# A gated delta rule in pairs of heads: the next pair's projection, issued one product at a time in other places of TensorE's order

## The reference

```python
# per head, with chunks of 128 tokens
A = jnp.where(strict, einsum(k_beta, kc) * L, 0.0)
sol = lax.linalg.triangular_solve(eye + A, rhs, lower=True, unit_diagonal=True)
u, w = sol[..., :dv], sol[..., dv:]
attn = jnp.where(causal, einsum(qc, kc) * L, 0.0)
def step(S, inp):
    v_new = u_n - w_n @ S
    o = q_n @ S + a_n @ v_new
    S = S * d_n + k_n.T @ v_new
    return S, o
...
do = do * lax.rsqrt(jnp.mean(do * do, axis=-1) + EPS) * dn_norm_g[l]
do = do.reshape(B, T, DN_V) * jax.nn.silu(dz)
y_dn = do @ w_dn_br[l]
merged = jax.nn.sigmoid(gate_r) * y_ret + jax.nn.sigmoid(gate_d) * y_dn
h = h + merged @ w_o[l]
```

## Time and profile before

| | us |
|---|---|
| median of 3 runs | 2510.35 (2509.15 to 2514.41) |
| profiled execution | 2510.26 |
| its span | 2508.3 |
| TensorE busy | 2352.5 (94%) |
| VectorE, ScalarE, GpSimd busy | 1132.0, 851.0, 871.7 |

### The profile page before, as it was taken

The page is one execution under the profiler, slowest core; times in us unless marked ns, Lnnn a source line. Parts: engine busy times, 40 slices in busy tenths (PEclk is TensorE's granted clock), DMA queues, the critical chain, the costliest instruction groups (busy, mean ns, idle before and its releaser), DMA issues.

```text
span 2508.3 us, 28287 instructions
## 1 busy us (share of the span) xinstructions
PE 2352.5 (94%) x11226; PEld 1908.3 (76%) x11226; DVE 1132.0 (45%) x1490; ACT 851.0 (34%) x844; POOL 871.7 (35%) x382
## 2 busy tenths in 40 slices
PE   7999999989899999999998999999997889999897
PEld 5888787757567788888776778878796867788786
DVE  7322007746644632200725416463737445877502
ACT  4222214357443422221426424141414033333312
POOL 3444343423213344434432434141322123344343
PEclk9999999999999999999999999999999889999998
DMA  4322223322322323222321132121111023222222
GB/s 137 97 88 92 84 92 90 87 56 69 108 73 71 108 86 99 92 76 95 108 78 57 60 101 84 34 72 46 48 54 59 26 98 110 87 92 92 67 92 76
DMA packets 161873, 203.23 MB, mean 81 GB/s; under 512 B 11949, under 2 KB 116728, under 8 KB 161784
## 3 DMA queue, kind: packets, MB, share of 16 engines
q1 hardware_dynamic: 155008, 197.16, 24.8%
q10 hardware_dynamic: 6775, 4.80, 0.6%
HBM read 191.45 MB, written 10.49 MB: 81 GB/s over the span
## 4 chain that ended last, share of the span: by engine, by line
PE 59%; issue 16%; DVE 15%; ACT 5%; POOL 4%; DMA 0%; SPq 0%; POOLq 0%; DVEq 0%; ACTq 0%
PE PS L167 15%; PE PS L168 15%; PE PS L169 15%; POOL wl L158 4%; DVE cv L2045 2%; PE PS L1911 2%; PE PS L1920 1%; DVE h_lo L310 1%; PE PS L1919 1%; PE PS L194 1%; PE PS L195 1%; PE PS L196 1%; PE PS L1007 1%; DVE work L2088 1%; DVE work L2078 1%
## 5 line engine op out<-in xcount | busy, mean ns | idle before, releaser
L158 POOL TENSOR_TENSOR wl<-raw,wh 128x2048 fp32r<-128x2048 f32 (+1 forms) x214 | 805.8, 3766 | 1487.3 <-ACT wh L149 1487.3
L167 PE MATMUL PS<-h_hi,wh 128*128 128x512 f32 x1696 | 680.1, 401 | 23.1 <-DVE h_lo L310 8.7
L169 PE MATMUL PS<-h_hi,wl 128*128 128x512 f32 x1696 | 666.6, 393 | 0.0
L168 PE MATMUL PS<-h_lo,wh 128*128 128x512 f32 x1696 | 666.1, 393 | 0.0
L149 ACT ACTIVATE wh<-raw 128x2048 fp32r<-128x2048 f32 (+1 forms) x214 | 340.0, 1589 | 935.1 <-PE PS L169 874.2
L167 PEld LDWEIGHTS PS<-h_hi,wh 128*128 128x128 f32 x1696 | 322.3, 190 | 104.1 <-issue 9.6
L169 PEld LDWEIGHTS PS<-h_hi,wl 128*128 128x128 f32 x1696 | 321.7, 190 | 69.2
L168 PEld LDWEIGHTS PS<-h_lo,wh 128*128 128x128 f32 x1696 | 322.7, 190 | 63.9 <-issue 0.7
L167 PE MATMUL PS<-act_hi,wh 128*128 (+1 forms) x528 | 210.0, 398 | 7.9 <-POOL wl L158 6.6
L616 DVE SCALAR_TENSOR_TENSOR xT<-PS,xT 128x512 f32<-128x512 f32 x40 | 27.4, 685 | 407.4 <-PE PS L169 407.3
L168 PE MATMUL PS<-act_lo,wh 128*128 (+1 forms) x528 | 209.5, 397 | 0.0
(11 more groups left out here) (439 smaller groups left out, 3114.9 us busy)
## 6 DMA issues: line engine op xcount, KB each, us to landing
raw<-in_w_in_dram SPq DMA_DIRECT2D x104, 512.0 KB, 4.7
raw<-in_w_up_dram SPq DMA_DIRECT2D x88, 512.0 KB, 4.8
raw<-in_w_down_dram SPq DMA_DIRECT2D x132, 256.0 KB, 2.8
raw<-in_w_gate_dram SPq DMA_DIRECT2D x44, 512.0 KB, 3.9
raw<-in_w_out_dram SPq DMA_DIRECT2D x16, 256.0 KB, 2.7
raw<-in_w_ret_br_dram SPq DMA_DIRECT2D x8, 512.0 KB, 4.8
gates<-stage SPq DMA_DIRECT2D x16, 256.0 KB, 5.5
raw<-in_w_dn_br_dram SPq DMA_DIRECT2D x8, 512.0 KB, 4.6
```

The source lines that it names most:

```text
L158: nc.gpsimd.tensor_tensor(wl[:, slot, 0:size], raw[:, slot, 0:size], wh[:, slot, 0:size].bitcast(F32), ALU.subtract).then_inc(w_lo, 1)
L167: nc.tensor.matmul(dst, sh, mh, start=start, stop=False)
L168: nc.tensor.matmul(dst, sh, ml, start=False, stop=False)
L169: return nc.tensor.matmul(dst, sl, mh, start=False, stop=stop)
```

## The change

`next_panel` takes a number of products and keeps its own place in the panel, so a k-step can be split. The 32 products of pairs 0 to 2 are dealt out as 2 in each of the six levels, 2 before `u`, 5 behind it, 1 before each of chunk steps 1 to 3, 7 behind the last chunk step and 3 behind `oT`. The second half of the pair's second panel is split by `panel_b`: 4 products before the wait on `silA`, 12 behind its transposes. In pair 3, 24 products of the branch product are dealt out (before: 16): 6 before the wait on `T0`, 1 in each level, 1 before `u`, 3 behind it, 1 before each of chunk steps 2 and 3, 6 behind the last. The units of `w_dn_br` come in another order (all of banks 0 to 3 first), and `merge2b_pe` has 40 products left: 4 behind `oy`, 36 behind `olo`. ScalarE rounds unit u+8 (in pair 3 ub+2) behind `uev` instead of before `u`, and u+9 behind `ohi` instead of behind `uev`.

```diff
--- before.py
+++ after.py
@@ -1716,17 +1716,30 @@
 
     def merge2b_sp(sp):
         for v in range(4):
-            panel(sp, ub + v, A['w_dn_br_2'][0], 4 * (v // 2), 4, 512 * (v % 2))
+            panel(sp, ub + v, A['w_dn_br_2'][0], 4 * (v % 2), 4, 512 * (v // 2))
             if v == 2:
                 wide_store(sp, WIDE - 1)
 
     def merge2b_pe(pe):
 
         await_point(pe, "dve", 3, "oy")
-        unit_T(pe, ub + 1, (ub + 1) % 2, 4, 0, 4, do_hi, do_lo, True, False)
+        branch_part(pe, ub + 2, 4, 0, 1)
         await_point(pe, "dve", 3, "olo")
-        unit_T(pe, ub + 2, (ub + 2) % 2, 0, 4, 4, do_hi, do_lo, False, True)
-        unit_T(pe, ub + 3, (ub + 3) % 2, 4, 4, 4, do_hi, do_lo, False, True)
+        branch_part(pe, ub + 1, 0, 6, KD)
+        branch_part(pe, ub + 2, 4, 1, 4)
+        branch_part(pe, ub + 3, 4, 4, KD)
+
+    def branch_part(pe, u, bank, k0, k1):
+
+        if k0 % 4 == 0:
+            pe.wait_ge(w_lo, u + 1)
+        for k in range(k0, k1):
+            for m in range(4):
+                c0 = (k % 4) * 512 + m * P
+                ins = mm3(PS[:, bank + m, :], wh[:, u % 2, c0:c0 + P], wl[:, u % 2, c0:c0 + P], do_hi[:, k, :], do_lo[:, k, :],
+                          k == 0, k == KD - 1)
+        if k1 % 4 == 0:
+            ins.then_inc(w_used, 1)
 
     def merge2b_load(act):
 
@@ -1762,7 +1775,7 @@
             dve.tensor_tensor(part, part, sig_r[:, 4 * n:4 * n + 4, :], ALU.mult).then_inc(g_mul, 1)
         for n in range(2):
             dve.wait_ge(g_sig, SIG1 + 3 + n)
-            dve.wait_ge(w_used, ub + 3 + n)
+            dve.wait_ge(w_used, ub + 2 + 2 * n)
             for m in range(4 * n, 4 * n + 4):
                 dve.tensor_tensor(sig_d[:, m, :], sig_d[:, m, :], PS[:, m, :], ALU.mult).then_inc(g_mul, 1)
             for m in range(4 * n, 4 * n + 5):
@@ -1853,12 +1866,13 @@
                 unit_T(pe, u + 1, (u + 1) % 2, 0, 4, 4, h_hi, h_lo, False, True)
                 pe.wait_ge(M1_copied, 2)
             unit_T(pe, u + 2, u % 2, 4, 0, 4, h_hi, h_lo, True, False)
+            panel_b(pe, u + 3, 4, 5)
             await_point(pe, "act", pp, "silA")
             for a in range(4):
                 for c in range(NT):
                     ins = pe.transpose(tile_of(PS, a, c), tile_of(cv, a, c), ident[:, :])
             at_point(ins, "pe")
-            unit_T(pe, u + 3, (u + 1) % 2, 4, 4, 4, h_hi, h_lo, False, True)
+            panel_b(pe, u + 3, 5, KD)
             await_point(pe, "dve", pp, "qn")
             for a, src in ((0, wE), (2, wkd)):
                 for e in range(2):
@@ -1899,9 +1913,11 @@
                 pe.wait_ge(fl_ev, GATES + q - KD + 2)
                 wide_mm(pe, q + 3, 3, 0, KD)
 
-            await_point(pe, "dve", pp, "T0")
             pe.wait_ge(fl_ev, GATES + q - KD + (4 if pp < 3 else 2))
             await_point(pe, "act", pp, "aT")
+            if pp == 3:
+                next_panel(pe, pp, 6)
+            await_point(pe, "dve", pp, "T0")
             for l, b in enumerate(LEVELS):
                 n = 2 * (len(LEVELS) * pp + l)
                 for e in range(2):
@@ -1910,7 +1926,7 @@
                     for c in range(NT):
                         ins = mm(tile_of(PS, 4 + e, c), tile_of(wAT, e, c), tile_of(wT, e, c), start=True, stop=True)
                     ins.then_inc(d_X, 1)
-                next_panel(pe, pp, l)
+                next_panel(pe, pp, 2 if pp < 3 else 1)
                 for e in range(2):
                     pe.wait_ge(d_Xm, n + e + 1)
                     for c in range(NT):
@@ -1920,7 +1936,7 @@
                         ins = mm(PS[:, 6 + e, 256 + lo:256 + hi], tile_of(wX, e, c), halves(tile_of(wU, e, c), b)[1],
                                  start=True, stop=True)
                     ins.then_inc(d_TU, 1)
-            next_panel(pe, pp, 6)
+            next_panel(pe, pp, 2 if pp < 3 else 1)
             pe.wait_ge(d_Um, 2 * len(LEVELS) * (pp + 1))
             pe.wait_ge(d_scaled, 3 * (pp + 1))
             for e in range(2):
@@ -1928,10 +1944,12 @@
                     mm(tile_of(PS, 4 + e, c), tile_of(wU, e, c), tile_of(wvb, e, c), start=True, stop=True)
                     ins = mm(tile_of(PS, 6 + e, c), tile_of(wkb, e, c), tile_of(wU, e, c), start=True, stop=True)
             at_point(ins, "pe")
-            next_panel(pe, pp, 7)
+            next_panel(pe, pp, 5 if pp < 3 else 3)
             await_point(pe, "act", pp, "uev")
             for c in range(NT):
                 if c:
+                    if pp < 3 or c > 1:
+                        next_panel(pe, pp, 1)
                     for e in range(2):
                         pe.wait_ge(d_S, 2 * (3 * pp + c - 1) + e + 1)
                         mm(PS[:, 6 + e, 0:P], tile_of(wAT, e, c), Sst[:, e, :], start=True, stop=True).then_inc(d_wS, 1)
@@ -1943,27 +1961,44 @@
                         mm(PS[:, 6 + e, P:2 * P], tile_of(wkd, e, c), tile_of(wX, e, c), start=True, stop=True).then_inc(d_kv, 1)
                     ins = mm(tile_of(PS, 4 + e, c), tile_of(waT, e, c), tile_of(wX, e, c), start=c == 0, stop=True)
             at_point(ins, "pe")
+            next_panel(pe, pp, 7 if pp < 3 else 6)
             await_point(pe, "dve", pp, "on")
             for e in range(2):
                 for c in range(NT):
                     ins = pe.transpose(tile_of(PS, 6 + e, c), tile_of(wT, e, c), ident[:, :])
             at_point(ins, "pe")
-
-    def next_panel(pe, pp, k):
-
-        if pp == 3 and k >= 4:
-            return
-        u = ud + 6 * pp + 6 + k // 4 if pp < 3 else ub
+            if pp < 3:
+                next_panel(pe, pp, 3)
+
+    def panel_b(pe, u, k0, k1):
+
+        if k0 == 4:
+            pe.wait_ge(w_lo, u + 1)
+        for k in range(k0, k1):
+            for m in range(4):
+                c0 = (k % 4) * 512 + m * P
+                ins = mm3(PS[:, 4 + m, :], wh[:, u % 2, c0:c0 + P], wl[:, u % 2, c0:c0 + P], h_hi[:, k, :], h_lo[:, k, :],
+                          k == 0, k == KD - 1)
+        if k1 == KD:
+            ins.then_inc(w_used, 1)
+
+    panel_at = [0, 0, 0, 0]
+
+    def next_panel(pe, pp, n):
+
         mh, ml = (h_hi, h_lo) if pp < 3 else (do_hi, do_lo)
-        if k % 4 == 0:
-            pe.wait_ge(w_lo, u + 1)
-        if pp == 3 and k % 2 == 0:
-            await_point(pe, "dve", k // 2, "olo")
-        for m in range(4):
+        for _ in range(n):
+            k, m = panel_at[pp] // 4, panel_at[pp] % 4
+            panel_at[pp] += 1
+            u = (ud + 6 * pp + 6 if pp < 3 else ub) + k // 4
+            if m == 0 and k % 4 == 0:
+                pe.wait_ge(w_lo, u + 1)
+            if pp == 3 and m == 0 and k % 2 == 0:
+                await_point(pe, "dve", k // 2, "olo")
             c0 = (k % 4) * 512 + m * P
             ins = mm3(PS[:, m, :], wh[:, u % 2, c0:c0 + P], wl[:, u % 2, c0:c0 + P], mh[:, k, :], ml[:, k, :], k == 0, k == KD - 1)
-        if k % 4 == 3:
-            ins.then_inc(w_used, 1)
+            if m == 3 and k % 4 == 3:
+                ins.then_inc(w_used, 1)
 
     def delta_pool(pool):
         los(pool, ud, 4)
@@ -2016,14 +2051,10 @@
                 wide_out(act, q + 2, 2)
                 wide_out(act, q + 3, 3)
                 rounds(act, u + 7, 1)
-                rounds(act, u + 8, 1)
-            else:
-                rounds(act, ub + 2, 1)
             await_point(act, "pe", pp, "u")
             act.activation(wX, PS[:, 4:6, :], ACT.Copy)
             at_point(act.activation(wAT[:, :, :], PS[:, 6:8, :], ACT.Copy), "act")
-            if pp < 3:
-                rounds(act, u + 9, 1)
+            rounds(act, u + 8 if pp < 3 else ub + 2, 1)
             await_point(act, "pe", pp, "o")
             if pp == 3:
                 merge2b_load(act)
@@ -2032,6 +2063,8 @@
             at_point(act.activation(ssq[:, 0:8], ssq[:, 0:8], ACT.Sqrt), "act")
             await_point(act, "dve", pp, "oy")
             at_point(act.activation(do_hi[:, 2 * pp:2 * pp + 2, :], wU, ACT.Copy), "act")
+            if pp < 3:
+                rounds(act, u + 9, 1)
 
     def conv(dve, pp, lo, hi, src):
```

## The result

| | us |
|---|---|
| before, median of 4 runs | 2510.61 (2509.15 to 2514.41) |
| changed, median of 4 runs | 2479.06 (2478.05 to 2479.84) |
| changed, profiled execution and its span | 2479.08, 2477.2 |

The ratio of the runs is 0.9872, with a 95% interval from 0.9855 to 0.9889: 31.5 us faster. The forecast was 2483 us, 27.7 us faster, with a range from 2474 to 2494.

The account below looks back on a forecast made before the run. TensorE's work plus its idle or half-clock stretches was taken to bound the kernel. Three boundaries 18.6, pair 0 -0.6, pair 3 15.3 and clock -5.6 sum to 27.7 us off 2510.35: 2483 us, range 2474 to 2494.

Parts of the forecast that it names:

- TensorE's stalls are filled by products that cover nothing where they stood: Pairs 0 to 2: products leave the levels and fill waits at the boundary, 6.2 us gained for each of three boundaries.
- From `oT` to `qn` nothing changes: Pair boundaries: VectorE's and ScalarE's steps set `qn`, a fixed 13.65 us behind the `silA` transposes; moving products out gains nothing.
- The split saves at `silA` what it pays at `qn`: The 2.56 us stall goes, idle before `qn` grows from 0.75 to about 3.5 us: zero; pair 0 loses 0.6 us.
- The clock behind the new gap: Behind `qn`: a 3.5 us idle gap, four times, brings half clock, 4 x 1.4 = 5.6 us lost.
- the rival in which the clock holds: Behind `qn`: the clock stays full through the new gaps; 2477 us, chance 0.24.
- GpSimd beside the convolution: nothing: Boundaries: GpSimd's subtraction beside the convolution costs zero, bounded above by 4.5 us per boundary.
- Pair 3: Last pair: 8.2 us gained up to its end, 5.6 from fewer products behind it, 1.45 from half clock; 15.3 us together.
- 2504 us: No-change rival: half clock behind each new gap lasts as long as pair 3's 13.7 us, 27 us lost; chance 0.03.
- the blocked convolution: Rival: GpSimd's subtraction blocks the convolution, three boundaries late by 4.5 us; 2496 us, chance 0.08.
- the late u+9: Rival: the convolution keeps GpSimd out, so u+9 delays the `silA` transposes, three times 5.4 us; 2499 us, chance 0.05.

Follow-up runs that it names:

- e6: e3 with the twelve products of the six levels in pairs 0 to 2 all moved ahead of the wait on `T0`, leaving those levels empty; 2460.57 us.
- e7: The kernel before with only the new deal of products in pairs 0 to 2 and the moved roundings of u+8 and u+9; 2490.27 us.
- e1: The changed kernel with the second panel's split undone, all 16 products behind the `silA` transposes; 2479.59 us.
- e2: The changed kernel with 2 products before the `silA` transposes and 14 behind, instead of 4 and 12; 2476.77 us.
- e10: The kernel before with only the second panel's split, 4 products before the `silA` transposes and 12 behind; 2521.10 us.
- e4: The changed kernel with the products of pairs 0 to 2 dealt out as in the kernel before; 2506.24 us.
- e3: The changed kernel with ScalarE rounding unit u+4 behind the root of the sums of squares instead of before it; 2459.31 us.
- e9: The kernel before with only ScalarE's rounding of unit u+4 moved behind the root of the sums of squares; 2507.45 us.
- e5: e3 with six products of pair 3 put ahead of `silB`, six kept ahead of `T0` and none in its levels; 2457.19 us.
- e8: e5 with ScalarE issuing pair 3's four gate loads behind the root `osd` instead of ahead of the square; 2448.99 us.

## Why the prediction was right

**TensorE's stalls are filled by products that cover nothing where they stood: right.** From `T0` to `oT` pair 1 went from 67.84 to 61.24 us (1684.24 to 1752.08 before, 1679.77 to 1741.01 after), 6.60 us where the sum had 6.2. e6 and e7 show the mechanism.

**From `oT` to `qn` nothing changes: right but for one term.** `silA` to `qn` was 13.65 us and is 13.64. `oT` to `silA` was 18.53 and is 17.60. The missed 0.93 us is `oT` itself, which stood at half clock behind the 4.31 us stall and lasts 1.04 us instead of 1.97. I looked at the half clock behind `oy`, where it was hidden, and passed over the transposes, where it was on the chain. Three boundaries: 2.8 us. The text of the prediction lets the closed gaps gain in clock too, "as summed above", but in pairs 0 to 2 the sum had no such term.

**The split saves at `silA` what it pays at `qn`: right**, by e1. In pair 0 it cost 0.4 us instead of 0.6: its `silA` transposes start 35.39 us behind the stage's first product (1469.90 to 1505.29), where it was 35.03 (1469.51 to 1504.54).

**The clock behind the new gap: right in kind.** It fell in all four pairs. `qn` to `T0` is longer by 1.15, 1.15, 1.49 and 1.45 us, 5.2 together, where the sum had 5.6. The reason that I gave, that 3.5 us lies nearer to 3.91 than to 2.56, was poor. The row of the 3.91 itself lasts 1.09 us for eight transposes, which is full clock, and only the 7.03 us behind it are followed by a slow one; e2 shows a fall after 2.25, and e10 none after 3.46. Since a gap of the same length didn't cost the clock there, that it did in four of four was partly luck. The time couldn't have told: 2479 us lies nearer to the rival in which the clock holds (2477) than to the forecast, and what decides against it are the clock of 0.95 and the longer stretches.

**GpSimd beside the convolution: nothing, right.** The convolution's sixteen instructions take 2.72 and 8.22 us beside a subtraction at 1746.35, as they did alone.

**Pair 3: 8.4 us from the first X to the products behind the pair (8.2 forecast), 6.8 us there (7.05).** The half clock gave back less: 29.74 us for 40 products against 28.0 at full rate is 1.7 us still lost of 2.9. No run has pair 3's part by itself, but e4 has it with the split and e10 has the split without it: 2506.24 against 2521.10 us, 14.9 us for it and the moved roundings, where the trace has 15.2 and the forecast 15.3.

Pairs 0 and 2 gained 6.53 and 6.55 us up to `oT` and 0.93 each behind it, so the terms as measured are 22.5 - 5.2 - 0.4 + 8.4 + 6.8 = 32.1 us; the span gave 31.1, and the rest lies outside the stage. The 3.8 us between forecast and result are the `oT` transposes (2.8), the way from `T0` to `oT` (1.1) and small terms both ways. One sum among the rivals was wrong: 2504 us with the blocked convolution or the late u+9 on top is 2517 to 2520 us, 0.3 to 0.4% slower than before, and not within 0.2%. Neither came.

What neither the profile before nor my reading made plain is how far the parts depend on each other. I booked the split at zero, and it is zero only beside this deal.

## What to carry to other kernels

An engine's wait is worth filling only if the chain that it waits for doesn't merely end somewhere else: follow it to the next wait on the same chain before counting the first. Work that is moved should come from a place where it covers nothing, which one comparison of the same step with and without it shows. And once the bound engine's stalls are filled, look again at short instructions with long times on the engines beside it; a stall that cost 3 us before can cost 20 after.

## What the runs showed of the hardware

- A VectorE TENSOR_SCALAR on 16 elements per partition, from SBUF to SBUF, took 4.10 us while GpSimd's subtraction ran and 0.17 us otherwise (e3, e9). The convolution's instructions, which have one operand in PSUM, took in the same company what they take without it (four TENSOR_SCALARs 2.72 us, twelve SCALAR_TENSOR_TENSORs 8.22).
- The granted clock fell behind gaps of 4.31, 3.60 (e1), 3.46 (changed) and 2.25 us (e2). It did not behind 2.56 in the kernel before, 3.46 in pair 3 of e10 and 3.60 in pair 1 of e7. A short gap isn't safe by itself, and a longer one doesn't always cost the clock.
- Four DMA issues in ScalarE's list took 2.5 us (1959.00 to 1961.55 in e5), and the square behind them waited for that long: with them behind the root, in e8, the wait before `oT` (2.71 us in e5) and the half clock behind it were gone.
